# Two layers of a hybrid encoder: products of the last stage in two groups, and the first layer's input read in place

## The reference

```python
def mixer_layer(h, w_in, ...):
    proj = jnp.matmul(h, w_in)
    ...
    a = mlstm_mixer(...)      # 4 heads x 64, chunkwise matrix memory, both directions
    b = gqa_mixer(...)        # 6 query heads, 2 key/value heads, full attention
    c = dilated_mixer(...)    # 6 heads in dilated windows
    mixed = jnp.concatenate([a, b, c], axis=-1)
    return jnp.matmul(mixed, w_out)

def trunk(x, norm_pre, w_in, ..., norm_post):
    for l in range(DEPTH):
        h = rms_norm(x, norm_pre[l])
        y = mixer_layer(h, w_in[l], ...)
        x = x + rms_norm(y, norm_post[l])
    return x
```

## Time and profile before

| | |
|---|---|
| time, median of 3 runs | 4430.91 us (4426.84 to 4438.43) |
| profiled execution: time / span | 4423.61 / 4421.8 us |
| mean granted TensorE clock | 0.939 of full speed |
| busy: PE / PEld / DVE / ACT / POOL | 88% / 78% / 51% / 45% / 28% |
| products of `finish` (L1926) | 3 x 576, idle before them 60.7 us |
| DMA | 488.06 MB, mean 110 GB/s |

### The profile page before, as it was taken

How to read it: one execution, slowest core, us unless ns; L and a number is a source line. 1 busy time by engine, 2 the same in 40 slices (tenths; PEclk the granted TensorE clock), 3 DMA queues, 4 the chain that set the end, 5 groups by cost and what they waited for, 6 DMA issues and landing times. The chain is left out here.

```text
span 4421.8 us, 59652 instructions
## 1 busy us (share of the span) xinstructions
PE 3873.9 (88%) x20480; PEld 3434.4 (78%) x20480; DVE 2259.7 (51%) x4159; ACT 1969.7 (45%) x3781; POOL 1251.5 (28%) x934
## 2 busy tenths in 40 slices
PE   3999999995499999868859999999955999989688
PEld 3999999993277777757759999999923777768566
DVE  4133311115688887766641333111056888868665
ACT  4133311104588787235541333101055787763354
POOL 0000000001177777435400000000012777764344
PEclk8999999997699999879979999999976999999899
DMA  5544412116611110965533443112175111119554
GB/s 193 140 132 128 130 65 78 62 68 223 175 35 31 36 34 13 243 163 162 152 120 97 136 136 119 69 62 78 53 259 146 29 36 36 31 41 244 153 171 136
DMA packets 489069, 488.06 MB, mean 110 GB/s; under 512 B 136720, under 2 KB 431856, under 8 KB 476656
## 3 DMA queue, kind: packets, MB, share of 16 engines
q1 hardware_dynamic: 488544, 483.93, 36.1%
q10 hardware_dynamic: 288, 1.05, 0.1%
HBM read 322.61 MB, written 171.70 MB: 112 GB/s over the span
## 5 line engine op out<-in xcount | busy, mean ns | idle before, releaser
L407 PE MATMUL pj_acc<-h_hi,pj_whi 128*128 128x384 f32 x2976 | 1007.1, 338 | 19.8 <-DVE pj_wlo L528 17.2
L407 PE MATMUL pj_acc<-h_lo,pj_whi 128*128 128x384 f32 x2976 | 997.8, 335 | 0.0
L407 PE MATMUL pj_acc<-h_hi,pj_wlo 128*128 128x384 f32 x2976 | 997.4, 335 | 0.0
L1340 POOL TENSOR_TENSOR ga_plo<-ga_prob,ga_phi 128x512 fp32r<-128x512 f32 (+1 forms) x594 | 766.2, 1300 | 415.5 <-ACT ga_prob L1305 402.0
L1017 POOL TENSOR_TENSOR rq_t<-rq_qn,rq_cos 128x1280 f32<-128x1280 f32 (+1 forms) x16 | 49.4, 3105 | 2212.1 <-DVE rq_qn L874 2212.1
L531 DVE TENSOR_SCALAR pj_stage<-pj_acc 128x384 f32<-128x384 f32 x186 | 113.6, 611 | 1088.3 <-PE pj_acc L407 1088.2
L1362 DVE TENSOR_REDUCE ga_mx<-ga_ps_x 128x1 f32<-128x512 f32 (+1 forms) x792 | 532.8, 680 | 177.8 <-PE ga_ps_x L1249 165.2
L407 PEld LDWEIGHTS pj_acc<-h_hi,pj_whi 128*128 128x128 f32 x2976 | 560.9, 188 | 20.6 <-DVE pj_wlo L528 17.7
L407 PEld LDWEIGHTS pj_acc<-h_lo,pj_whi 128*128 128x128 f32 x2976 | 560.8, 188 | 0.0
L407 PEld LDWEIGHTS pj_acc<-h_hi,pj_wlo 128*128 128x128 f32 x2976 | 560.5, 188 | 0.0
L1303 ACT ACTIVATE ga_phi<-ga_ps_s 128x512 fp32r<-128x512 f32 (+1 forms) x792 | 469.2, 592 | 193.8 <-PE ga_ps_s L1266 186.3
(11 more groups left out here) (187 smaller groups left out, 6201.5 us busy)
## 6 DMA issues: line engine op xcount, KB each, us to landing
proj<-pj_stage SPq DMA_DIRECT2D x44, 1152.0 KB, 4.4
pj_w<-in_w_in SPq DMA_DIRECT2D x62, 512.0 KB, 4.3
dl_kv<-dil_kv SPq DMA_DIRECT2D x108, 256.0 KB, 2.9
ml_qk<-mqk SPq DMA_DIRECT2D x72, 384.0 KB, 5.2
fi_z<-proj SPq DMA_DIRECT2D x36, 640.0 KB
pn_x<-y SPq DMA_DIRECT2D x36, 512.0 KB, 4.5
ml_mb<-gate_M SPq DMA_DIRECT2D x72, 256.0 KB, 4.9
ml_kv<-tokmaj SPq DMA_DIRECT2D x72, 256.0 KB, 5.0
```

The costliest lines, as they stand in the source:

```text
L407: mm = pe.matmul(acc[s % 2][:, 0:CHUNK], wt[u][:, t, :], ht[:, t, tok], start=(t == 0 and i == 0), stop=(t == KT - 1 and i == 2))
L1340: vector.tensor_tensor(p_lo[r][:, 0:w], prob[f % 2][:, 0:w], p_hi[r][:, 0:w].bitcast(F32), ALU.subtract).then_inc(sem, 1)
```

## The change

The copy of `x_all` into `y` is left out, with its share of SP's wait. In layer 0, `pre_norm` and `finish` read x from `x_all`, in layer 1 from `y`; `finish` stores to `y` in both. In `multiply`, a half is now 16 products with the mix's high part (with the high and the low part of the weights by turns), after a wait for `hi_ok`, and then 8 with the mix's low part, after a wait for `lo_ok`. The wait ahead of the tile goes.

```diff
--- before.py
+++ after.py
@@ -170,6 +170,8 @@
             k.sem("pn_" + s) for s in ("gain_in", "stats", "rstd_ok", "h_ok", "turned", "hi_ok", "lo_ok"))
         block = ctx.enter_context(nc.Block())
 
+        x_now = k.a["y" if L else "x_all"]
+
         def number(b, u):
             return (L * NB + b) * NU + u
 
@@ -182,7 +184,7 @@
                 for u in range(NU):
 
                     sp.wait_ge(h_ok, number(b, u) + 1)
-                    sp.dma_start(x[u][:], k.a["x"][tokens(b, u), :]).then_inc(x_in[u], DMA)
+                    sp.dma_start(x[u][:], x_now[tokens(b, u), :]).then_inc(x_in[u], DMA)
 
         @block.scalar
         def _(act):
@@ -1717,12 +1719,12 @@
                     sp.dma_start(dl[u][:, g].rearrange("p h e -> p (h e)"), seq[at(j0, P // dil)]).then_inc(s, DMA)
 
             def load_x(b, c):
-                sp.dma_start(x[c % 2][:], rows_of(k.a["x"], (b * 2 + c) * P, P, 0, D_MODEL)).then_inc(x_in[c % 2], DMA)
+                sp.dma_start(x[c % 2][:], rows_of(k.a["y" if L else "x_all"], (b * 2 + c) * P, P, 0, D_MODEL)).then_inc(x_in[c % 2], DMA)
 
             def slot(b, c):
                 if exists(b, c - 1):
                     sp.wait_ge(x_ok, number(b, c - 1) + 2)
-                    sp.dma_start(rows_of(k.a["x"], (b * 2 + c - 1) * P, P, 0, D_MODEL), xo[(c - 1) % 2][:]
+                    sp.dma_start(rows_of(k.a["y"], (b * 2 + c - 1) * P, P, 0, D_MODEL), xo[(c - 1) % 2][:]
                                  ).then_inc(stored[(c - 1) % 2], DMA)
                     if exists(b, c + 1):
                         load_x(b, c + 1)
@@ -1921,17 +1923,19 @@
 
             def multiply(b, c, half):
                 u, cols_ = c % 2, slice(half * 512, (half + 1) * 512)
+                pe.wait_ge(hi_ok, number(b, c) + 1)
                 for t in range(KT):
-                    for i, (a, w) in enumerate(((m_hi, w_hi), (m_lo, w_hi), (m_hi, w_lo))):
-                        mm = pe.matmul(ps_y[u][:, cols_], a[u][:, t, :], w[:, t, cols_],
-                                       start=(t == 0 and i == 0), stop=(t == KT - 1 and i == 2))
+                    for i, w in enumerate((w_hi, w_lo)):
+                        pe.matmul(ps_y[u][:, cols_], m_hi[u][:, t, :], w[:, t, cols_], start=(t == 0 and i == 0), stop=False)
+                pe.wait_ge(lo_ok, number(b, c) + 2)
+                for t in range(KT):
+                    mm = pe.matmul(ps_y[u][:, cols_], m_lo[u][:, t, :], w_hi[:, t, cols_], start=False, stop=(t == KT - 1))
                 return mm
 
             def slot(b, c):
                 if exists(b, c + 1):
                     turn_o(b, c + 1)
                 if exists(b, c):
-                    pe.wait_ge(lo_ok, number(b, c) + 2)
                     multiply(b, c, 0)
                 if exists(b, c + 1):
                     turn_heads(b, c + 1)
@@ -1996,7 +2000,6 @@
 
     with ExitStack() as ctx:
         k = Kernel(nc, ctx, arrays)
-        k.a["x"] = k.a["y"]
         k.dram("proj", (NCT, P, TOK))
 
         k.dram("mqk", (6, P, TOK))
@@ -2030,10 +2033,9 @@
 
             @block.sync
             def _(sp):
-                sp.dma_start(k.a["x"], k.a["x_all"]).then_inc(once, DMA)
                 sp.dma_start(ident_t[:], k.a["ident"]).then_inc(once, DMA)
                 sp.wait_ge(filled, 3)
-                sp.wait_ge(once, 2 * DMA)
+                sp.wait_ge(once, DMA)
 
             @block.scalar
             def _(act):
```

## The result

| | before | after |
|---|---|---|
| median of 5 runs | 4433.38 us (4426.84 to 4441.73) | 4400.78 us (4392.16 to 4406.82) |
| profiled execution: span | 4421.8 us | 4399.0 us |
| mean granted clock | 0.939 | 0.940 |

The ratio is 0.9922, with a 95% interval of 0.9902 to 0.9943: 25 to 43 us faster. The median fell by 32.6 us, against 33.5 us in the prediction. That the two lie within 1 us of each other is closer than these runs can tell; whether the sum was right is read from its parts.

The account below looks back on a forecast made before the run. The prediction took the copy to bound the start and the load loop the middle of `finish`. 29.1 (start) + 0 (middle) + 4.4 (tails) = 33.5 us off 4430.9 gave 4397.4 us, range 4387 to 4409.

Parts of the forecast that it names:

- The copy was all path: Start: `ident` waits behind the copy on SP's queue; without it the first x load is issued 29.1 us earlier.
- The 0.8 us from wait to issue: Start: from the end of SP's wait for `ident` to its issue of the first x load, 0.8 us.
- rule on code fetches: Start: a branch outside the fetched window stalls; part of the 29.1 us could come back, by an unpriced amount.
- The products gave only the tails: Last tiles of `finish` in each layer: TensorE starts earlier, 4.4 us in sum, bounds 1 and 5.7.
- the clock dip staying away: Layer 0's tail: of up to 3.1 us gained, about 1.4 come only without the clock dip; 2.7 taken.
- The middle gave nothing: Steady part of `finish`: reordered products bring nothing, within 0.1 us a period either way, +-3 us; period still 14.2 us.
- what is late next is the load: Steady part of `finish`: the load loop, a turn of 14.59 us, ends last, not TensorE.
- the two waits that the prediction named: `finish`: TensorE waits for `fi_e` (sigmoid) and `fi_mhi` (cast) in place of the low part, nearly the same sum.
- TensorE's work a tile: `finish`: two halves of products, 11.2 us, and seven transposes, some 0.8 more: 12.0 us.
- Wait in the loop: Rival, `finish`: each low-part wait removed shortens the kernel, about 59 us, with the start 88: 4343 us; chance 0.03.
- Something else behind the copy: Rival, start: an engine isn't ready at 3.9 us; 29.1 us lost, 4426.5 us, chance 0.02; half lost, 4412 us, 0.02.
- Clock: Rival, `finish`: split idle time keeps TensorE's clock low, a tile takes 21.1 us, 4632 us in all; chance 0.01.

Follow-up runs that it names:

- the copy alone: Kernel after with the products in the old order, so only the copy removed: 4405.6 us, 0.9936 of the kernel before.
- the products alone: Kernel before with only the products reordered, the copy kept: 4428.4 us, 0.9999 of the kernel before.
- gate load first: Kernel after with a semaphore of its own for the load of the gate columns: 4382.3 us; the same with the old product order: 4391.0 us.
- both: Kernel after with the gate columns' own semaphore and VectorE's low part moved into the next tile's normalising: 4353.9 us; with the old product order: 4449.8 us.
- low part late: Kernel after with VectorE's low part moved behind the first half of the next tile's normalising: 4387.9 us, 0.9886 of the kernel before.
- 8 more products: Kernel after with four more products ahead of each half, their sum overwritten: 4401.8 us, 0.9938 of the kernel before.

## Why the prediction was right

- **The copy was all path.** 29.1 us forecast, 29.5 found at the first x load, 29.0 at `project`, 28 by the time of the copy alone. The 0.8 us from wait to issue held; `ident` landed in 1.9 us, not 2.3. Nothing else had been standing behind the copy. The Trainium skill's rule on code fetches (Runtime: NRT & Kernel Launch, "Instruction fetch mechanics"), by which part of it might have come back, cost nothing that the trace shows: from the end of SP's wait to its first x load it takes 0.9 us, 0.8 before.
- **The products gave only the tails.** 4.4 us forecast, 3.8 by the stage's length, 4.2 over four kernels. Layer 1: 1.7 forecast, 1.67 found. Layer 0: 2.7 forecast, 2.38 found, and this nearness is partly luck. I had put 1.4 of the 3.1 us down to the clock dip staying away. But the half took 2208.34 - 2201.38 = 6.96 us with the dip; started at 2198.75 it ends at 2205.71, a gain of 2.6 us with the whole dip in it. The dip did come again (the first product has 0.80 us, the half 7.16), so the rows had held 2.6 for this case, not 1.7.
- **The middle gave nothing**, 14.17 against 14.18. Right in what it says, but "what is late next is the load" was only half of it: the chain of ACT and VectorE stood less than 0.5 us behind. ACT's 17.5 us in 16 waits bounded that distance at 1.1 us a tile; the runs put it at 0.35 (14.17 - 13.82).
- **One wait was left out.** TensorE was to wait for the sigmoid or the cast instead; the largest share, 11.4 of 26.2 us, is the head scaling ahead of the second half. So the two waits that the prediction named have 14.8 us, not nearly the 29.4 it asked for as a sign. It costs nothing, since TensorE has time to spare.
- **TensorE's work a tile** was put at 12.0 us and measured at 11.5: 0.233 us a product counts the slow first one in (0.228 without it), and the rest is the transposes' modelled end.
- **The rivals.** Wait in the loop: excluded by the products alone. Something else behind the copy: excluded by the 29.0 us at `project`. Clock: it went the other way, below.

## What to carry to other kernels

A wait is worth what it holds up, not what it lasts: 59 us of TensorE's waiting gave 4 us. An edit without gain that loosens an order may be the condition for the next one: the low part could move only because its user had become patient, and the best kernel with the new order is 37 us faster than the best with the old one. Two loops of nearly the same length must both be shortened. A large copy holds up the loads behind it on its queue, awaited or not; here, in 64 KB rows, it held them up on another queue too. So it has to be removed, or moved to where no load is urgent (this last was not tried).

## What had not been expected of the hardware

**Granted clock.** Before, in the middle of each layer's `finish` (columns as above):

```profile
1990.00:2150.00 160.00, 140.98 (x626) 113.67 (x626) 111.37 (x195) 93.61 (x138) 80.77 (x45) 0.97 0.54 163
4170.00:4340.00 170.00, 148.83 (x661) 119.91 (x660) 116.67 (x204) 98.18 (x144) 83.22 (x47) 0.97 0.54 161
```

and after:

```profile
1990.00:2150.00 160.00, 140.19 (x621) 107.48 (x620) 112.42 (x192) 93.37 (x137) 83.87 (x45) 1.00 0.55 170
4170.00:4340.00 170.00, 148.78 (x661) 114.35 (x660) 118.46 (x204) 98.04 (x144) 86.89 (x48) 1.00 0.55 165
```

With the wait for the low part TensorE had one idle piece of up to 2.8 us in a tile, and the clock fell to its lower level (1.2 GHz) for some products after some of them: 0.97 of full speed in both stretches. With the idle time in three pieces of mostly under 1 us it was 1.00 in both. In the same two stretches the other kernels with the old order had 0.96 and 0.97 (copy only), 0.98 and 0.98 (gate load first) and 0.95 and 0.93 (both); those with the new order 1.00 and 0.98 (products only), 1.00 and 0.97 (low part late) and 1.00 in both (8 more products, gate load first, both). So the new order has the higher clock in layer 0 throughout, but it can fall there too. That the length of the single idle pieces decides is argued from this, not tested by itself. TensorE had time to spare, so this moved nothing here. The rule of the Trainium skill that I had weighed against the change (TensorE: Matmul & The Clock Gate, "Why this matters for your kernels"), that idle gaps between bursts bring the low clock back, points the same way as these rows: it spoke for the change.

**VectorE beside POOL.** The low part took 2.57 us in the mean beside POOL's product and 1.22 where POOL was idle, the log-sigmoid 2.51 beside the residual. In the period of the earlier trace rows:

```profile
4230.92 2.36 POOL L1750 TENSOR_TENSOR fi_z<-fi_z,fi_e 128x1024 f32<-128x1024 f32 x1 [2.73 <-ACT fi_e L1792]
```

The product ends at 4233.28, and 1.22 us more is 4234.50; the low part ended at 4234.35. The Trainium skill (SBUF — State Buffer, "Who interferes with whom") says that the two engines share a pair of ports which one instruction holds to its end, and that this concerns a VectorE instruction with two inputs in SBUF, such as the low part, beside a GpSimd instruction that reads SBUF. The low part's end agrees with waiting for POOL to within 0.2 us.
